# RWKV stage: token mixing split between ACT and DVE, keys ahead of the low-rank products, low-rank products in pairs on the row halves of PE

## What is computed

```python
prev = concatenate([shift0[:, None, :], p[:, :-1]], axis=1)     # the row before
xs = p + mu * (prev - p)                                        # token mixing, 1792 columns
r, k, v, xw, xa, xg = split(xs, ...)                            # 512, 512, 512, 64, 64, 128
w = -softplus(-(w0 + tanh(xw) @ w2)) - 0.5                      # low-rank products
a = sigmoid(a0 + xa @ a2)
g = sigmoid(xg) @ g2
kk = heads(k * k_k)
kk = kk / maximum(norm(kk, axis=-1, keepdims=True), 1e-12)
k = k * (1.0 + (a - 1.0) * k_a)
...                                                             # delta-rule scan over the tokens, then norm, bonus, gate
```

## Time and profile before

| | us |
|---|---|
| median of 3 runs | 2072.12 |
| lowest, highest | 2071.74, 2072.6 |
| the profiled execution | 2065.0 |
| its span, first to last instruction | 2063.1 |
| PE busy in the span | 1784.8 |
| DVE busy | 1486.1 |
| ACT busy | 1025.1 |

### The profile page before, as it was taken

The page is one execution under the profiler, slowest core; times in us unless marked ns, Lnnn a source line. Parts: engine busy times, 40 slices in busy tenths (PEclk is TensorE's granted clock), DMA queues, the critical chain, the costliest instruction groups (busy, mean ns, idle before and its releaser), DMA issues. The chain is left out here.

```text
span 2063.1 us, 27607 instructions
## 1 busy us (share of the span) xinstructions
PE 1784.8 (87%) x10224; PEld 1305.3 (63%) x10224; DVE 1486.1 (72%) x1326; ACT 1025.1 (50%) x885; POOL 162.0 (8%) x165
## 2 busy tenths in 40 slices
PE   3499999964885980999999999999999999999970
PEld 0144577632783440777778787777878778787750
DVE  0164355366754441899999999999999999999955
ACT  1011222232230230777777777777777777777741
POOL 0000000001300204010000000000000000000006
PEclk7699999966897985999999999999999999999985
DMA  9830311500001417899999999999999999999736
GB/s 378 335 127 36 108 47 51 220 23 26 22 5 61 152 58 251 310 370 380 367 377 393 362 383 363 382 368 380 387 364 380 366 379 389 360 387 362 307 122 240
DMA packets 116954, 535.26 MB, mean 259 GB/s; under 512 B 15048, under 2 KB 16980, under 8 KB 82811
## 3 DMA queue, kind: packets, MB, share of 16 engines
q1 hardware_dynamic: 102048, 491.06, 61.3%
q0 software_dynamic: 7680, 25.31, 3.3%
q10 hardware_dynamic: 7162, 18.01, 2.2%
HBM read 498.41 MB, written 35.89 MB: 259 GB/s over the span
## 5 line engine op out<-in xcount | busy, mean ns | idle before, releaser
L1926 DVE TENSOR_TENSOR ex_weights_lo<-weight_ring,ex_weights_hi 128x2048 fp32r<-128x2048 f32 x256 | 574.2, 2285 | 19.3 <-ACT ex_weights_hi L1861 17.7
L1861 ACT CAST ex_weights_hi<-weight_ring 128x2048 fp32r<-128x2048 f32 x256 | 486.4, 1914 | 151.1 <-PE banks L2034 91.6
L2013 PE MATMUL banks<-ex_weights_hi,ex_rows_hi_lo 128*128 128x512 f32 x2048 | 516.0, 394 | 1.4 <-ACT ex_weights_hi L1861 1.4
L2013 PEld LDWEIGHTS banks<-ex_weights_hi,ex_rows_hi_lo 128*128 128x128 f32 x2048 | 381.3, 189 | 92.5 <-issue 12.7
L1931 DVE TENSOR_TENSOR ex_weights_lo<-weight_ring,ex_weights_hi 128x2048 fp32r<-128x2048 f32 x128 | 293.0, 2293 | 53.3 <-ACT ex_weights_hi L1868 53.3
L1868 ACT CAST ex_weights_hi<-weight_ring 128x2048 fp32r<-128x2048 f32 x128 | 244.7, 1914 | 101.3 <-PE banks L2013 101.3
L2013 PE MATMUL banks<-ex_weights_lo,ex_rows_hi_lo 128*128 128x512 f32 x1024 | 275.1, 391 | 0.0
L2034 PE MATMUL banks<-ex_weights_hi,ex_rows_hi_lo 128*128 128x512 f32 x1024 | 259.0, 395 | 2.6 <-ACT ex_weights_hi L1868 2.6
L2034 PEld LDWEIGHTS banks<-ex_weights_hi,ex_rows_hi_lo 128*128 128x128 f32 x1024 | 190.9, 189 | 55.1 <-issue 13.2
L2013 PEld LDWEIGHTS banks<-ex_weights_lo,ex_rows_hi_lo 128*128 128x128 f32 x1024 | 193.3, 189 | 40.4
L2034 PE MATMUL banks<-ex_weights_lo,ex_rows_hi_lo 128*128 128x512 f32 x512 | 137.7, 391 | 0.0
(11 more groups left out here) (326 smaller groups left out, 1761.8 us busy)
## 6 DMA issues: line engine op xcount, KB each, us to landing
weight_ring<-in_moe_w_gu SPq DMA_DIRECT2D x256, 1024.0 KB, 8.5
weight_ring<-in_moe_w_down SPq DMA_DIRECT2D x128, 1024.0 KB, 10.1
weight_ring<-in_w_ada SPq DMA_DIRECT2D x8, 3072.0 KB, 30.3
expert_rows<-ex_plain ACTq DMA_DIRECT2D x32, 512.0 KB
weight_ring<-in_w_in SPq DMA_DIRECT2D x6, 2048.0 KB, 20.5
expert_rows<-arena SPq DMA_DIRECT2D x16, 512.0 KB
weight_ring<-in_cache_k SPq DMA_DIRECT2D x24, 256.0 KB, 3.2
weight_ring<-in_cache_v SPq DMA_DIRECT2D x24, 256.0 KB, 3.3
```

The costliest lines, as they stand in the source:

```text
L1861: nc.scalar.copy(hi_of(i), raw_chunk(m, i)).then_inc(q["gu_hi"], 1)
L1926: V.tensor_sub(lo_of(i), raw_chunk(m, i), plain(hi_of(i))).then_inc(q["gu_lo"], 1)
L2013: last = T.matmul(m.bank[n], x[:, i, :], w[:, n * 512:(n + 1) * 512], start=False, stop=(i == GU - 1 and w is lo))
```

## The change

Token mixing is written as (row before) times mu plus (current row) times (1 - mu). ACT makes the first product into the destination, 14 of them (`before`); DVE adds the second with one operation for each tile (`mix`), with `keep` = 1 - mu. ACT makes the products for `xl` and k first, then tanh and sigmoid, then the copies of the shift rows; the products for r and v alternate with its sigmoids. DVE makes `kk` and its square right behind k, without the wait for the low-rank products. PE makes the eight 64-row products of 512 columns in turn on rows 0 to 63 and 64 to 127, each into a bank of its own, then all 8-column ones, then those for `g` with theirs behind them. `xl` moves from the arena to the weight ring, where it shares space with `v_tok`.

```diff
-        b_tok, k_tok, v_tok, a_tok = (w.take(NT, AW) for _ in range(4))
+        b_tok, k_tok = (w.take(NT, AW) for _ in range(2))
+        v_tok_at, v_tok, a_tok = w.at, w.take(NT, AW), w.take(NT, AW)
+        xl = w.whole[:, v_tok_at:v_tok_at + 2 * TOK].rearrange("p (n t) -> p n t", n=2)
...
         @block.scalar
         def _(act):
+            def before(dst, f0, f):
+
+                nc.scalar.activation(dst[:, f, 0:SEQ], m.pp[:, f0 + f, 0:SEQ], ACT.Copy,
+                                     scale=par[:, MU + f0 + f:MU + f0 + f + 1]).then_inc(q["before_mixed"], 1)
+
+            act.wait_ge(q["params_done"], 1)
+            for f in range(2):
+                before(xl, 12, f)
+            for f in range(4):
+                before(k, 4, f)
+            act.wait_ge(q["mixed_lora"], 1)
+            nc.scalar.activation(xl[0:HD, 0, :], xl[0:HD, 0, :], ACT.Tanh).then_inc(q["lora_act"], 1)
+            nc.scalar.activation(xl[:, 1, :], xl[:, 1, :], ACT.Sigmoid).then_inc(q["lora_act"], 1)
             act.wait_ge(q["shift_psum"], 1)
...
+            for i in range(2 * PAIRS):
+                h, dst, bias0 = i // 2, (sw, ga)[i % 2], (W0, A0)[i % 2]
+                act.wait_ge(q["lora_mm"], i + 1)
+                nc.scalar.activation(dst[:, h, cols[0]], m.bank[i][:, :], ACT.Sigmoid,
+                                     bias=par[:, bias0 + h:bias0 + h + 1]).then_inc(q["gates_done"], 1)
+                before((r, v)[i // 4], (0, 8)[i // 4], i % 4)
+            act.wait_ge(q["lora_mm"], 2 * PAIRS + 1)
...
+            for h in range(PAIRS):
+                act.wait_ge(q["lora_mm"], 2 * PAIRS + 2 + h)
+                nc.scalar.copy(g[:, h, cols[0]], m.bank[2 + h][:, :]).then_inc(q["gates_done"], 1)
...
-                V.tensor_sub(dst[:, :, 0:SEQ], m.pp[:, f0:f0 + nf, 0:SEQ], m.pp[:, f0:f0 + nf, 1:SEQ + 1]).then_inc(q["own"], 1)
...
+            def mix(dst, f0, nf, begun):
+
+                V.tensor_add(dst[:, :, SEQ:TOK], sh[:, f0:f0 + nf, :], cur_s[:, f0:f0 + nf, :])
                 for f in range(nf):
...
+                    dve.wait_ge(q["before_mixed"], begun + f + 1)
+                    last = V.scalar_tensor_tensor(dst[:, f, 0:SEQ], m.pp[:, f0 + f, 1:SEQ + 1], keep[:, f0 + f:f0 + f + 1],
+                                                  dst[:, f, 0:SEQ], ALU.mult, ALU.add)
+                return last
+
+            mix(xl, 12, 2, 0).then_inc(q["mixed_lora"], 1)
+            link(mix(k, 4, 4, 2))
             for h in range(PAIRS):
                 last = V.tensor_scalar(kk[:, h, :], k[:, h, :], par[:, KK_ + h:KK_ + h + 1], None, ALU.mult)
             link(last)
             V.tensor_mul(tmp_a, kk, kk).then_inc(q["kk_sq"], 1)
+            link(mix(r, 0, 4, 6))
+            mix(v, 8, 4, 10).then_inc(q["mixed_rkv"], 1)
...
-            pe.wait_ge(q["shift_copied"], 4)
             pe.wait_ge(q["lora_in"], 48)
             pe.wait_ge(q["lora_act"], 2)
             pe.wait_ge(q["params_done"], 1)
...
+            halves = (slice(0, HD), slice(HD, P))
+            for i in range(2 * PAIRS):
+                h, rows = i // 2, halves[i % 2]
+                if i == 2:
+                    pe.wait_ge(q["shift_copied"], 4)
+                T.matmul(m.bank[i][:, :], lora_wa[rows, h * P:(h + 1) * P], xl[rows, 0, cols[0]], start=True,
+                         stop=True).then_inc(q["lora_mm"], 1)
+            pe.wait_ge(q["gates_done"], 2)
...
+            for h in range(PAIRS):
+                pe.wait_ge(q["gates_done"], h + 3)
+                T.matmul(m.bank[2 + h][:, :], lora_g[:, h * P:(h + 1) * P], xl[:, 1, cols[0]], start=True,
+                         stop=True).then_inc(q["lora_mm"], 1)
...
             pe.wait_ge(q["kk_sq"], 1)
-            pe.wait_ge(q["gates_done"], 3 * PAIRS)
+            pe.wait_ge(q["gates_done"], 3 * PAIRS + 2)
```

More of the change, by code:

```diff
@@ L770, in rwkv @@
         sw = a.take(PAIRS, TOK)
-        kk_at = a.at
         kk = a.take(PAIRS, TOK)
         par_rows = a.take(P, rows=N_PAR)
-        a.at = kk_at
-        xl = a.take(2, TOK)
         a.at = nn_at
@@ L891, in _ @@
                 nc.scalar.copy(shift_rows[:, n * 512:n * 512 + c], m.bank[2 + n][0:NB + 1, 0:c]).then_inc(q["shift_copied"], 1)
[L892 to L905, removed]
+            for i in range(2 * PAIRS):
[6 more added lines that the diff above has]
+            for i in range(2 * PAIRS):
+                h, dst, bias0 = i // 2, (sw, ga)[i % 2], (W0, A0)[i % 2]
+                last = nc.scalar.activation(dst[:, h, cols[1]], m.bank[i % 2][:, h * NB:(h + 1) * NB], ACT.Sigmoid,
+                                            bias=par[:, bias0 + h:bias0 + h + 1])
+            last.then_inc(q["gates_done"], 1)
+            for h in range(PAIRS):
+                act.wait_ge(q["lora_mm"], 2 * PAIRS + 2 + h)
+                nc.scalar.copy(g[:, h, cols[0]], m.bank[2 + h][:, :]).then_inc(q["gates_done"], 1)
+            act.wait_ge(q["lora_mm"], 3 * PAIRS + 2)
+            nc.scalar.copy(g[:, :, cols[1]], m.bank[6][:, 0:PAIRS * NB].rearrange("p (h b) -> p h b", h=PAIRS))\
+                .then_inc(q["gates_done"], 1)
             act.wait_ge(q["kk_sum"], 1)
@@ L988, in _ @@
             link(V.tensor_mul(sh, sh, par[:, MU:MU + RF].unsqueeze(2).broadcast_to([P, RF, NB])))
-            for dst, f0, nf, done in ((xl, 12, 2, q["mixed_lora"]), (k, 4, 4, None), (r, 0, 4, None), (v, 8, 4, q["mixed_rkv"])):
-                V.tensor_sub(dst[:, :, 0:SEQ], m.pp[:, f0:f0 + nf, 0:SEQ], m.pp[:, f0:f0 + nf, 1:SEQ + 1]).then_inc(q["own"], 1)
[L991 to L994, removed]
-                for f in range(nf):
[L996 to L1004, removed]
+            dve.wait_ge(q["params_done"], 1)
+            def mix(dst, f0, nf, begun):
+                V.tensor_add(dst[:, :, SEQ:TOK], sh[:, f0:f0 + nf, :], cur_s[:, f0:f0 + nf, :])
+                for f in range(nf):
+                    dve.wait_ge(q["before_mixed"], begun + f + 1)
[4 more added lines that the diff above has]
+            link(mix(k, 4, 4, 2))
             for h in range(PAIRS):
```

27 lines of the change are left out of this document (16 added, 11 removed).

## The result

| | us |
|---|---|
| before, median of 8 runs on the same chip | 2070.64 (2064.96 to 2073.99) |
| changed, median of 8 runs | 2057.51 (2054.36 to 2062.07) |
| ratio, 95% interval | 0.9934 [0.9919, 0.9949] |
| profiled execution of the changed kernel, its span | 2057.82, 2056.0 |

The change makes the kernel faster by 13.7 us (2070.64 times 0.0066), with an interval of 10.6 to 16.8. The forecast was 2058.5.

A forecast was written before the change was run, and what follows sets the result against it. The stage's start was bound by DVE's chain, with an 11.0 us wait for PE and ACT's low-rank turns. Key norms at 451.05 instead of 464.65 gain 13.6: 2072.1 becomes 2058.5 us, range 2053.5 to 2066.5.

The forecast's parts named there:

- ACT first: Start of the rwkv stage: ACT makes six mixing products at 0.62 us each, PE begins at 428.75, only about 0.3 earlier.
- The turns: ACT alternates eight sigmoids and r or v products, 0.60 + 0.62 us each, 9.75 in all, and sets the pace.
- Chain one: DVE from scan, begun at 441.4, to its first key-norm instruction: 8.79 us as before, so 450.2.
- mark: DVE's first instruction on the key norms (L1021 before), where two chains end; forecast 451.05 instead of 464.65, 13.6 us earlier.
- Chain two: ACT's small sigmoids and g copies, then PE's head sums and ACT's square root of the norms: 450.6 to 451.4.
- Pairs: On PE, two 64-row products on different row halves run together, costing 1.84 us a pair at half clock, not 3.68.
- The rival of serial halves: PE's row halves run one after the other: gain 5.9 us, 2066.2; chance 0.08, plus 0.04 with no clock rise.
- The clock: PE's clock rises from half to full by about 444, during g's products; a rise already in the pairs gives 450.6.
- Taken back later: Rival: the later solve's dense PE stretch loses its warm clock; 10 us at 0.50 would leave 3.6 gain; chance 0.08.
- a warm spread: PE's spread behind the key norms (7.17 us at half clock) running at a raised clock: 1.3 us more gain.
- The profiled execution: The profiled run's time falls from 2065.0 to 2051.4, with the median of the runs staying 7.1 us higher.

The follow-up runs named there:

- lora_first: Changed kernel with ACT's four products for k moved behind tanh and sigmoid of the low-rank inputs; median 2054.24 us, ratio to before 0.9922.
- serial_halves: Changed kernel with PE's eight wide 64-row products reordered, four on rows 0 to 63, then four on 64 to 127; median 2055.59 us, ratio to before 0.9937.
- v_on_dve: Changed kernel with the four products for v taken from ACT, DVE mixing v itself; medians 2052.20 and 2050.70 us, ratios to before 0.9914 and 0.9906.
- halves_apart: Changed kernel with four products on rows 0 to 63 first, PE waiting for the fourth before the fifth; median 2060.04 us, ratio to before 0.9952.

## Why the prediction was right, step by step

- *ACT first.* A product was taken at 0.62 between 0.5 and 1.15; six take 3.69 or 0.61 each. PE began 7.07 after the stage's start where 7.31 were forecast. In lora_first it began 5.59 after, 1.5 earlier, and the scan came no earlier for it; only the first two products could start then, the third waited for the shift copies. The 0.96 for a 64-row product at full clock was read from a 128-row one; the 64-row records of serial_halves at 1.00 start 0.43 apart, 0.86 a product, so that was close.
- *The turns.* First sigmoid 9.15 after the start (9.41 forecast), then 1.18 a turn in place of 1.22: eight end at 18.62 in place of 19.2. The scan came at 19.56, forecast 19.96. ACT is the pace: the waits of DVE for its products are short, and with four products fewer (v_on_dve) the scan comes 2.0 earlier.
- *Chain one.* 8.79 from scan to mark, exactly. This chain set the mark in the profile after, 28.35 against 28.8.
- *Chain two.* Forecast root at 29.2 to 30.0; it came at 27.99 and, the second time, at 29.10. The eight small sigmoids took 1.19 and not 1.6; the head sums and root 5.8 against 6.15, the sums themselves 4.95 against the 5.29 of the earlier trace rows. The gain of 14.86 at the mark against 13.6 is these terms, and nothing else moved: from the mark to the end of the stage it is 194.93 before and 195.13 after.
- *Pairs.* They cost one product's time, not two, as the overlap in the earlier trace rows had it: the 5.78 for eight, and the 6.4 that halves_apart loses. The cleanest case is lora_first, where the last three pairs ran at 0.50 nearly throughout and took 5.35, about 1.8 each, against the 1.84 of a single product. The rival of serial halves was priced at a gain of 5.9; halves_apart, which is that kernel, gained 8.4 at the mark (43.21 less 34.77).
- *The clock.* A rise by about 444 on the axis of before is 22.6 after the start; it came at 11.3 (438.8), in the pairs themselves, the case for which 450.6 was forecast. The Trainium skill, "TensorE: Matmul & The Clock Gate", Part 1, has the throttled clock as the default that sustained activity releases. The pairs bear that out, with 0.50 and then 1.00 while PE was busy throughout; the same products one half at a time do not, with 0.50 over 15.8 us at a busy share of nearly 1 (halves_apart). Why the one released it and the other didn't, no run here shows.
- *Taken back later.* From mark to stage end it is 193.6 to 197.2 in all thirteen profiles, whatever the mark: the solve behind takes nothing back beyond that. The 1.3 that a warm spread was to give in the forecast's own range stands on no row; the spread took 7.17 at 0.50 in the profile after, as before.
- *The time.* That the 13.6 of the forecast is met to 0.1 us by the 13.7 of the result is closer than its working can claim, and partly luck. The interval is 10.6 to 16.8, the mark gained 14.86 in one profile of the changed kernel and 14.01 in the other, and the forecast of 2058.5 started from a median of three runs that lies 1.5 above that of all eight.
- *The profiled execution* was forecast at 2051.4 and came at 2057.82. The step that failed is that it would keep its distance of 7.1 to the median. 6.10 of it are the earlier start of the stage in that one profile, behind an attention stage at a higher clock; the other profiles started later. The median, 2057.51 for 2058.5, was not touched by it.

What stays open: whether the runs of v_on_dve are faster by more than its mark, by 5.2 give or take 3.1 where the mark is 2.0 and 2.8 earlier than in the two profiles of the changed kernel. The span behind the stage is 1401.1 and 1401.7 in its profiles and 1405.0 and 1404.1 in those of the changed kernel, but over all thirteen it goes from 1401.1 to 1406.5, and no edit touches it. What sets the clock of the attention stage is open too.

## What to carry to other kernels

When two chains meet at one instruction, count both after the edit: the one that was early (here the root) becomes the bound as soon as the other is shortened. What a part is worth then depends on the others: the early keys brought 7.5 as the only part, and 4.0 as the last of three. Work moved to an idle engine is free only until that engine paces the stage, so move back what it doesn't need to hold; here four of the fourteen products were better left on DVE. Compare profiles from the start of the stage, not of the span: a stage ahead of it, unchanged, moved by 6 us between two executions.

## What the hardware showed that was not expected

Products on the two row halves of PE overlap even where the list gives all of one half first (serial_halves: four and then eight records start within 3.5 us, at 0.52 and 0.50). The Trainium skill, "TensorE: Matmul & The Clock Gate", Part 3, says that products start and end in program order with no reordering; the starts here do not agree, the order in which the counts were handed on does.

The same eight records of the head sums took 4.95 and 6.05 in two executions of one program, behind 4.11 and 4.12 us of idle time, 6.54 behind 2.22 (lora_first), and 3.59 in v_on_dve and halves_apart, behind 1.79 and 0.37. So a gap on PE has a range for a price, not one number, even where the gap is the same.
